# Pair products of a gated linear recurrence that stream only the queries of second halves

## The reference

```
a = RMSNorm(h); z = a @ W_in
h += concat[HGRN2 | GatedDeltaNet | ConformerConv | MultiScalePool](z) @ W_out
h += PEER(RMSNorm(h))
h += sigmoid(RMSNorm(h) @ W_gate) * (p @ W_ple)
```

```
diff = la[:, :, :, None] - la[:, :, None, :]              # query t minus key s
dec = exp(where(causal, diff, NEG_BIG))
scores = einsum('bnthk,bnshk,bntshk->bnhts', q, k, dec)
```

## Time and profile before

| | |
|---|---|
| median of 3 runs | 4000.57 us (4000.55 to 4011.9) |
| span of the profiled execution, first to last instruction | 3988.8 us |
| its own time beside the span | not listed; the span is 11.8 us below the median of the runs |
| mean granted clock of TensorE | 0.983 |
| pair products, layer 0 and layer 1 | 159 to 240 us, 2133 to 2214 us |

### The profile page before, as it was taken

One profiled execution on the slowest core, in us unless ns is written; L12 is line 12 of the kernel. 1 busy time (PEld: TensorE's weight loads), 2 busy tenths in 40 slices (PEclk: granted clock), 3 DMA queues, 4 the chain that ended last, 5 costly groups with the idle time before them and its releaser, 6 DMA issues.

```text
span 3988.8 us, 59456 instructions
## 1 busy us (share of the span) xinstructions
PE 3877.4 (97%) x23204; PEld 3461.4 (87%) x23204; DVE 2869.6 (72%) x4841; ACT 1540.6 (39%) x2349; POOL 2259.3 (57%) x1452
## 2 busy tenths in 40 slices
PE   8999999999999999999999999999999999999999
PEld 6778599999999999999477876999999999999994
DVE  5764368955887878888567552799458887798885
ACT  1443145553333334444314432555532333343343
POOL 0032069887777657668101310888877774688861
PEclk9988999999999999999999899999999999999999
DMA  4201146666899999999221021566679899999992
GB/s 122 52 13 48 43 170 215 214 233 218 305 322 320 316 361 388 395 395 343 78 66 39 12 75 43 188 214 210 220 246 312 304 322 333 346 383 380 378 340 71
DMA packets 417975, 900.99 MB, mean 226 GB/s; under 512 B 94496, under 2 KB 242208, under 8 KB 416032
## 3 DMA queue, kind: packets, MB, share of 16 engines
q1 hardware_dynamic: 272288, 552.91, 40.2%
q0 software_dynamic: 90112, 268.76, 18.7%
q10 hardware_dynamic: 55296, 75.52, 5.2%
HBM read 773.87 MB, written 123.15 MB: 225 GB/s over the span
## 4 chain that ended last, share of the span: by engine, by line
PE 52%; POOL 15%; DMA 14%; DVE 11%; issue 5%; ACT 2%; SPq 0%; DVEq 0%; ACTq 0%; POOLq 0%
PE banks L1364 11%; PE banks L826 7%; PE banks L1376 7%; POOL peer_gates L2079 6%; PE banks L1438 5%; DMA u_stage<-peer_ut 5%; POOL u_stage L2095 4%; PE banks L1473 4%; DMA gated<-dense_gelus 3%; PE banks L1275 3%; POOL u_stage L2087 3%; DMA peer_gates<-peer_v,u_stage 3%; PE banks L1293 3%; DVE normed L2729 2%; DMA normed<-peer_ut 1%
## 5 line engine op out<-in xcount | busy, mean ns | idle before, releaser
L2079 POOL DMA_INDIRECT peer_gates<-peer_v,u_stage x512 | 733.8, 1433 | 387.3 <-DVE normed L2729 157.6
L1438 PE MATMUL banks<-gated_parts,v_parts 128*128 128x320 f32 x6144 | 911.1, 310 | 19.9 <-DVE gated_parts L2776 18.2
L1438 PEld LDWEIGHTS banks<-gated_parts,v_parts 128*128 128x128 f32 x6144 | 905.8, 189 | 25.4 <-issue 25.2
L1364 PE MATMUL banks<-peer_x_parts,u_parts 128*128 128x448 f32 x3168 | 664.0, 367 | 3.3 <-DVE u_parts L2715 3.3
L1364 PEld LDWEIGHTS banks<-peer_x_parts,u_parts 128*128 128x128 f32 x3168 | 590.5, 188 | 49.6 <-DVE u_parts L2715 4.1
L2095 POOL DMA_INDIRECT u_stage<-dense_gelus,u_stage x256 | 374.5, 1463 | 106.9 <-issue 77.4
L1364 PE MATMUL banks<-peer_x_parts,low_s 128*128 128x448 f32 x1696 | 398.3, 367 | 0.5 <-DVE low_s L2715 0.5
L2729 DVE SCALAR_TENSOR_TENSOR normed<-peer_gates,u_stage,normed 128x1024 f32<-128x1024 f32 x254 | 327.5, 1289 | 85.3 <-DMA peer_gates<-peer_v,u_stage 71.0
L2745 DVE SCALAR_TENSOR_TENSOR peer_gates<-peer_gates,u_stage 128x1024 f32<-128x1024 f32 x254 | 325.4, 1281 | 81.3 <-DMA peer_gates<-peer_v,u_stage 71.3
L1869 ACT ACTIVATE u_stage<-banks 128x448 f32<-128x448 f32 x256 | 139.2, 544 | 621.8 <-PE banks L1364 616.8
L2087 POOL DMA_INDIRECT u_stage<-gelus,u_stage x256 | 329.0, 1285 | 78.1 <-issue 78.0
(11 more groups left out here) (355 smaller groups left out, 6642.6 us busy)
## 6 DMA issues: line engine op xcount, KB each, us to landing
v_stage<-peer_v SPq DMA_DIRECT2D x256, 512.0 KB, 7.7
u_stage<-peer_ut SPq DMA_DIRECT2D x244, 512.0 KB, 5.2
dense_gelus<-u_stage ACTq DMA_DIRECT2D x256, 224.0 KB, 5.3
gates<-peer_gates SPq DMA_DIRECT2D x16, 2560.0 KB, 20.3
u_stage<-gates SPq DMA_DIRECT2D x64, 640.0 KB, 8.9
gated<-dense_gelus SPq DMA_DIRECT2D x256, 160.0 KB, 7.6
x<-peer_ut SPq DMA_DIRECT2D x64, 512.0 KB, 4.7
u_raw<-peer_ut SPq DMA_DIRECT2D x64, 512.0 KB, 4.9
```

What stands on the lines that cost most here:

```text
L1364: ins = mm(PS[:, d % 2, 0:DW], u_part(n, a, k), XR[:, b, k, DENSE0:TOK], start=(k == 0 and m == 0), stop=(k == KT - 1 and m == 2))
L1438: ins = mm(vc[k][:, 0:PW3], VR[:, s, b, k * 128:(k + 1) * 128], HR[:, s, a, :], start=(j == 0 and m == 0), stop=(j == NKEYS - 1 and m == 2))
L2079: eng.indirect_dma_start(out=GU[:, t % 4, :], out_offset=None, in_=din["peer_v"].rearrange("l i j d -> (l i j) d"), in_offset=bass.Indirec ...
```

## The change

For units from 2 on, TensorE streams only the queries of second halves: 64 of 128 columns a head, picked by a strided view (`second_halves`: runs of 2^l, every other one). The products of the four prompt tiles, 4 x 2 x 64 columns, now fill one bank, with one signal for all; the sample tile (2 x 32 columns) has a second bank at levels 0 to 2. VectorE copies each head's half-width products of all four tiles with one copy_predicated, so again two a unit, each of 4 x 64 elements a partition instead of 512; the output and the mask are strided views, and the bank is read as runs (`in_runs`). Keys, their scaling, the exponentials and units 0 and 1 stay. Waits that named a unit's last bank name the new last one.

```diff
--- before.py
+++ after.py
@@ -588,7 +588,20 @@
 
     def unit_banks(u):
         l, c, T = unit_of(u)
-        return 3 if T == TOK else 2
+        return 3 if l is None else 2 if T == TOK else 1
+
+    def second_halves(t, l):
+
+        w = 1 << l
+        if len(t.shape) == 2:
+            return t.rearrange("p (n g w) -> p n g w", g=2, w=w)[:, :, 1, :]
+        return t.rearrange("p h (n g w) -> p h n g w", g=2, w=w)[:, :, :, 1, :]
+
+    def in_runs(t, l):
+
+        if len(t.shape) == 2:
+            return t.rearrange("p (n w) -> p n w", w=1 << l)
+        return t.rearrange("p h (n w) -> p h n w", w=1 << l)
 
     def halo(t, c, width, halo_w, step, shift=0, n=SEQ):
 
@@ -901,6 +914,18 @@
                 else:
                     pe.wait_ge(pool_done, at("k_low", L, u))
                     pe.wait_ge(dve_done, at("q_low", L, u))
+                    pe.wait_ge(*bank_free())
+                    b = fill("hsc", L, u, 0).rearrange("p (i h t) -> p i h t", i=4, h=2)
+                    for i in range(SAMPLE):
+                        cols = slice(COL[i], COL[i] + 128)
+                        ins = mm(in_runs(b[:, i], l), left[:, c, cols], second_halves(QP[:, c, :, cols], l), start=True, stop=True)
+                    pe.did(ins.then_inc(pe_done, 1), "filled", "hsc", L, u, 0)
+                    if T == TOK:
+                        pe.wait_ge(*bank_free())
+                        b = fill("hsc", L, u, 1)[0:SAM, 0:SAM].rearrange("p (h t) -> p h t", h=2)
+                        ins = mm(in_runs(b, l), left[:, c, SEQ:TOK], second_halves(QP[:, c, :, SEQ:TOK], l), start=True, stop=True)
+                        pe.did(ins.then_inc(pe_done, 1), "filled", "hsc", L, u, 1)
+                    return
                 for two in range(2):
                     pe.wait_ge(*bank_free())
                     b = fill("hsc", L, u, two).rearrange("p (i h t) -> p i h t", i=2, h=2)
@@ -908,11 +933,10 @@
                         cols = slice(COL[2 * two + n], COL[2 * two + n] + 128)
                         ins = mm(b[:, n], left[:, c, cols], QP[:, c, :, cols], start=True, stop=True)
                     pe.did(ins.then_inc(pe_done, 1), "filled", "hsc", L, u, two)
-                if T == TOK:
-                    pe.wait_ge(*bank_free())
-                    b = fill("hsc", L, u, 2)[0:SAM, 0:2 * SAM].rearrange("p (h t) -> p h t", h=2)
-                    ins = mm(b, left[:, c, SEQ:TOK], QP[:, c, :, SEQ:TOK], start=True, stop=True)
-                    pe.did(ins.then_inc(pe_done, 1), "filled", "hsc", L, u, 2)
+                pe.wait_ge(*bank_free())
+                b = fill("hsc", L, u, 2)[0:SAM, 0:2 * SAM].rearrange("p (h t) -> p h t", h=2)
+                ins = mm(b, left[:, c, SEQ:TOK], QP[:, c, :, SEQ:TOK], start=True, stop=True)
+                pe.did(ins.then_inc(pe_done, 1), "filled", "hsc", L, u, 2)
 
             def decayed_turned(i):
 
@@ -2020,7 +2044,7 @@
                 pool.did(eng.tensor_tensor(halves(KLOW[:, c], l, T)[:, :, 0, :], halves(KF[:, c], l, T)[:, :, 0, :],
                                            halves(EE[:, u % 2], l, T)[:, :, 0, :], ALU.mult).then_inc(pool_done, 1), "k_low", L, u)
             pool.wait_ge(act_done, at("vt", L))
-            pool.wait_ge(pe_done, at("filled", "hsc", L, HUNITS - 1, 1))
+            pool.wait_ge(pe_done, at("filled", "hsc", L, HUNITS - 1, 0))
             for h in range(4):
                 pool.did(eng.tensor_tensor(VM[0:SAM, h], bc(VT[0:SAM, SAMPLE, h * 64:(h + 1) * 64], 1, NB),
                                            bc(member_s[0:SAM], 2, 64), ALU.mult).then_inc(pool_done, 1), *(("vm", L) if h == 3 else ()))
@@ -2356,6 +2380,19 @@
                 l, c, T = unit_of(u)
                 if l is not None:
                     dve.wait_ge(dve_done, at("drained", "hsc", L, u - 2, unit_banks(u - 2) - 1))
+                    ups = second_halves(const("ups")[:, l * 128:(l + 1) * 128], l).bitcast(U32)
+                    dve.wait_ge(pe_done, at("filled", "hsc", L, u, 0))
+                    b = bank("hsc", L, u, 0).rearrange("p (i h t) -> p i h t", i=4, h=2)
+                    for hh in range(2):
+                        ins = eng.copy_predicated(second_halves(ST[:, :, 2 * c + hh, :], l), bc(ups, 1, 4), in_runs(b[:, :, hh], l))
+                        dve.did(ins.then_inc(dve_done, 1), *(("drained", "hsc", L, u, 0) if hh else ()))
+                    if T == TOK:
+                        ups = second_halves(const("ups")[0:SAM, l * 128:l * 128 + SAM], l).bitcast(U32)
+                        dve.wait_ge(pe_done, at("filled", "hsc", L, u, 1))
+                        b = bank("hsc", L, u, 1)[0:SAM, 0:SAM].rearrange("p (h t) -> p h t", h=2)
+                        ins = eng.copy_predicated(second_halves(SST[0:SAM, 2 * c:2 * c + 2, :], l), bc(ups, 1, 2), in_runs(b, l))
+                        dve.did(ins.then_inc(dve_done, 1), "drained", "hsc", L, u, 1)
+                    return
                 for two in range(unit_banks(u)):
                     dve.wait_ge(pe_done, at("filled", "hsc", L, u, two))
                     b = bank("hsc", L, u, two)
@@ -2367,11 +2404,7 @@
                         out = SST[0:SAM, 2 * c:2 * c + 2, :]
                         b = b[0:SAM, 0:2 * SAM].rearrange("p (h t) -> p h t", h=2)
                         over = lambda m: bc(m[0:SAM, 0:SAM], 1, 2)
-                    if l is None:
-                        ins = TT(out, b, over(ident), ALU.mult)
-                    else:
-                        ins = eng.copy_predicated(out, over(const("ups")[:, l * 128:(l + 1) * 128].bitcast(U32)), b)
-                    dve.did(ins.then_inc(dve_done, 1), "drained", "hsc", L, u, two)
+                    dve.did(TT(out, b, over(ident), ALU.mult).then_inc(dve_done, 1), "drained", "hsc", L, u, two)
 
             def conv(c):
 
@@ -2414,7 +2447,7 @@
                 if u % 2 and 3 <= u < 15:
                     conv((u - 3) // 2)
             counts.same(("conv", L), ("qr_ready", L, 5))
-            counts.same(("hst", L), ("drained", "hsc", L, HUNITS - 1, 1))
+            counts.same(("hst", L), ("drained", "hsc", L, HUNITS - 1, 0))
             step_state(0)
             def sample_state():
```

## The result

| | before | changed | ratio, 95% interval |
|---|---|---|---|
| first measurement, 22 runs each | 4013.24 us (3991.17 to 4036.83) | 3995.72 us (3971.96 to 4010.07) | 0.995 (0.9934 to 0.9966) |
| second, 17 and 12 runs | 4004.97 us | 3983.68 us | 0.9953 (0.9933 to 0.9973) |
| third, 23 and 12 runs | 4013.6 us | 3996.42 us | 0.9945 (0.9924 to 0.9965) |

The change makes the kernel about 0.5% faster, three times over. The medians of the first measurement differ by 17.5 us; 17.4 were forecast. The time itself, 3995.72 us, lies outside the range of 3976 to 3992, because the kernel before took 4013 us there and not the 4000.57 on which the sum stood.

The account below looks back on a forecast made before the run. TensorE's streaming was taken to bound the pair-product stage: 9.4 us a layer, 18.9 for two, less 1.5 for the clock, gives 17.4 us off 4000.57, so 3983.2 us; forecast 3978 to 3987, range 3976 to 3992.

Parts of the forecast that it names:

- Term 1, streaming: Prompt-tile products of units 2 to 11: records fall from 0.216 to 0.111 us, saving 8.35 us a layer.
- term 2, the sample tile: Levels 0 to 2, 64 instead of 128 streamed columns: two records save 0.07 us, 0.4 us a layer.
- The rival of strided reads: TensorE's short strided runs cost: levels 0 and 1 gain nothing, 3990 us (chance 0.08), or outweigh the halving, 4012 (0.05).
- That of a record bound by its weight load: Pair products: no streaming gain, only the tail's 0.7 us a layer, 3999 us; chance 0.03.
- Term 3, the tail: After the last feature tile: unit 12's shorter copies start unit 15's decay earlier, ScalarE then limits; gain 0.69 us a layer.
- The sum of the path: Pair-product stage and tail: 8.35 + 0.4 + 0.69 = 9.4 us a layer saved, before the clock's loss.
- Hidden edits: VectorE's copies off the path: 0.36 us each, leaving VectorE 1.1 us of slack in a cycle of two units.
- VectorE as releaser inside the stage: Sign that the prediction is wrong: VectorE, not TensorE, releasing work within the pair-product stage; no size given.
- Term 4, the clock: Sums of squares after the stage: TensorE idles more, its clock may fall earlier; loss 1.5 us over both layers, bounds -3 and +5.

Follow-up runs that it names:

- before_again: The kernel before the change, unedited, traced once more; first product to state step 83.2 us in each layer, as before.
- contiguous: Changed kernel with TensorE's half-width products reading the first 64 columns a head (32 for the sample tile) in one run; first product to state step 73.8 us a layer.
- quarter: Changed kernel with only 32 columns a head streamed for the prompt tiles, weight loads kept; 0.106 to 0.108 us a record, 73.5 us to state step.
- products_twice: Changed kernel with each half-width product issued twice into the same place, VectorE's copies kept halved; first product to state step 84.5 us a layer.
- copies_twice: Changed kernel with VectorE's half-width copies of the prompt tiles made twice, the second pair behind a wait; first product to state step 80.1 us a layer.
- late_twice_timed: Changed kernel with the prompt products of units 13 to 15 issued twice, timed with a second trace; ratio to before 0.9949 (0.9924 to 0.9973).

## Why the prediction was right, and where it was wrong

**The step that failed is the base of the sum**, the time before of 4000.57 us, from which the 17.4 were taken. It was the median of three runs; the median of 22, these three among them, is 4013.24. That is 12.7 us more, and 4013.24 less 17.4 is 3995.8, where 3995.72 was measured. The range of 3976 to 3992 had room for the rivals of the change and none for this, although the prediction itself says that a measurement tells 12 us from no change. How much of the scatter belongs to the chip stays open: the second and third measurement, on two chips, have before at 4004.97 and 4013.6.

Beside it stands a misreading that cancels in the sum. "The profiled execution's span is 3988.8 us, 11.8 below the median of the runs" was taken as time that lies outside the span. It is not: for the changed kernel the profiled execution has 3997.22 us with a span of 3995.4, and before_again 3985.48 with 3983.6, so 1.8 or 1.9 us lie outside. By that the traced execution of before took, as an estimate, 3991 us, near the fastest of the 22 runs (3991.17). A difference of 10 us between an execution and the median of the same code should have told me how far single numbers scatter.

**Term 1, streaming, and term 2, the sample tile.** From unit 2 to the end of the last feature tile before took 59.43 us (171.77 to 231.20 in the earlier trace rows), after 50.81. That is 8.62 against 8.35 + 0.4. Short records take 0.111 to 0.114, at level 0 0.119; the sample tile's two take 0.26 to 0.27 (I had 0.29). The rival of strided reads falls by contiguous. That of a record bound by its weight load falls by the change itself, and quarter puts the floor just below the new step.

**Term 3, the tail.** 0.73 us against 0.69. The two copies of unit 12 take 0.72 us to the next start (224.78 to 225.50), as assumed, and ScalarE bounds the rest. In products_twice, with the old streaming, this gain is gone.

**The sum of the path.** 9.3 us a layer (83.2 to 73.9) against 9.4 before the clock's term.

**Hidden edits: right in effect, wrong in size.** I took 0.36 us for a copy at all levels, argued from a product whose short runs cost nothing. Setting level 0 beside level 2 could not have shown a price that both bear, as they do for the copy (0.79 and 0.76 us). The 0.36 holds from level 5 on. At levels 0 to 2 copies start 0.57 us apart (two in 1.15, 174.03 to 175.18), near the upper bound. The slack, too, was read in one cycle, that of level 4, and taken for all. The first cycle of before, with sample tiles in it, was fuller; its window, in the columns of the earlier trace rows:

```profile
171.77:184.11 12.34, 12.34 (x54) 9.32 (x53) 10.76 (x22) 3.83 (x8) 2.61 (x2) 1.00 0.12 42
```

VectorE was busy for 10.76 of 12.34 us there, and TensorE's new cycle lasts 10.59. After the change VectorE is busy for 9.90 of these and for 10.14 of the next 10.62, which leaves 0.7 and 0.5 us, against 1.2 and 1.3 at levels 3 and 4. The sign that the prediction names as one of being wrong, VectorE as releaser inside the stage, did come, for 0.09 us in the second cycle. copies_twice shows how close it was.

**Term 4, the clock.** The sums of squares and the state step took 15.1 + 2.1 us over both layers in the changed kernel's first trace, 12.7 + 1.4 before: 3.2 lost where I took 1.5, within the bounds. The 40 records at the lower clock took 7.57 us, above the 7.3 that the prediction set as their top. To the output product the three traces of the change take 326.1 to 332.0 us over both layers, the two of before 321.3 and 326.3, some 6 us more on average. Whether that belongs to the change is not settled: late_twice_timed, with more work there, took longest.

**Together.** 18.6 us from the path, less 3 to 6 for the clock, is 13 to 16; the three measured differences are 17.5, 21.3 and 17.2, with intervals of 6 to 8 us on either side. They agree within these. That the first stands 0.1 us from the forecast 17.4 is luck: the clock cost more than its term, and the measurement can't tell so small a difference.

## What to carry to other kernels

Where the chain of a stage holds one engine and its steps go by the column, a record of the new shape elsewhere in the trace prices the edit to a few per cent; look there for the floor too, here 0.106 us a record however few columns it streams. Forecast the difference, and give the time itself a range as wide as executions of the same code scatter; a traced execution far from the median of the runs is a sign of that scatter. A stride that is free for one operation need not be for another, so bound it by the full cost and see what slack is left, in the fullest cycle and not in one that is typical.

## What the runs showed of the hardware that was not expected

- VectorE's copy_predicated pays for short output runs: the record of 256 elements a partition takes 0.79 us in runs of one or two, 0.76 in runs of four, 0.58 in eight, 0.51 in sixteen, 0.47 in 32, and 0.46 written in one run; from start to start it is 0.57 in runs of one, 0.36 in 32 and 0.35 written in one run. The mask's runs don't matter; the reading of the bank was not varied. VectorE's tensor_tensor over the same halves shows no such price: 0.45 us for 288 elements at levels 0 and 2, 0.42 for 256 at levels 3 and 5.
- The 115 row gathers of GpSimd in the pass over peer_v have a median issue time of 0.96, 1.23 or 1.63 us, by the execution, and the pass takes 458, 466 to 470 or 477 us with them.
- Behind a rest of 3.5 us TensorE ran the state step and all 40 records of 2 columns at a granted clock of 0.50, 0.19 us each, in eight of eight layers; behind 0.3 us they took 0.12 to 0.15, in four of four; behind 1.4 to 2.5 us either happened.
